# A two-layer trunk kernel: gate rows and routing weight products behind the first expert, first splits between the sort's copies, silu for the expert values

## The reference, cut to what matters

```python
sh1, sc1, g1, sh2, sc2, g2 = modulation(cond, w_mod, b_mod)    # six rows of D per layer and token kind
h2 = rmsnorm(x, norm2_g) * (1 + sc2) + sh2
pg = softmax(h2 @ w_rg + b_rg); pg_top, g_idx = top_k(pg, 1)   # one of 4 groups
le = (h2 @ w_re + b_re).reshape(-1, 4, 4)                       # 4 experts a group
pe_top, e_idx = top_k(softmax(le[group]), 2)                    # 2 experts of the group
combine[t, e] = pe_top / sum(pe_top) * pg_top
hid = silu(h2 @ w_eg[e]) * (h2 @ w_eu[e])                       # for every e of 16, width 256
x = x + g2 * sum_e (hid * combine[:, e]) @ w_ed[e]
```

## Time and profile before

| | |
|---|---|
| median of 3 runs | 2925.8 us (2925.13 to 2928.38) |
| profiled execution | 2934.5 us, span of the trace 2932.6 us |
| PE busy | 2620.1 us (89%) |
| PE weight loads | 1946.5 us (66%) |
| DVE busy | 1571.4 us (54%) |
| ACT busy | 1275.3 us (43%) |
| POOL busy | 38.7 us (1%) |
| read from HBM | 683.6 MB, mean 235 GB/s over the span |
| mean granted clock of PE | 0.936 |

### The profile page before, as it was taken

One profiled execution on the slowest core, in us unless ns is written; L12 is line 12 of the kernel. 1 busy time (PEld: TensorE's weight loads), 2 busy tenths in 40 slices (PEclk: granted clock), 3 DMA queues, 4 the chain that ended last, 5 costly groups with the idle time before them and its releaser, 6 DMA issues. The chain is left out here.

```text
span 2932.6 us, 33895 instructions
## 1 busy us (share of the span) xinstructions
PE 2620.1 (89%) x12386; PEld 1946.5 (66%) x12387; DVE 1571.4 (54%) x2039; ACT 1275.3 (43%) x1720; POOL 38.7 (1%) x68
## 2 busy tenths in 40 slices
PE   6799778999999899888988987789999989798897
PEld 1488434888887475666766873468888868476675
DVE  0444323455454343688885443245454555378887
ACT  0244233434443232666764433334344433267675
POOL 0000000000000002000000000000000000200000
PEclk7799988999999898999988999899999999799998
DMA  9654886555555658678774559755555535368875
GB/s 392 250 194 165 335 322 270 186 189 185 185 190 188 270 203 315 230 290 313 291 273 149 195 211 359 295 227 185 191 185 177 199 110 194 132 231 310 310 295 219
DMA packets 115640, 690.00 MB, mean 235 GB/s; under 512 B 24748, under 2 KB 30668, under 8 KB 32944
## 3 DMA queue, kind: packets, MB, share of 16 engines
q1 hardware_dynamic: 115504, 688.08, 63.2%
HBM read 683.58 MB, written 4.46 MB: 235 GB/s over the span
## 5 line engine op out<-in xcount | busy, mean ns | idle before, releaser
L880 DVE TENSOR_TENSOR low_w<-raw_w,high_w 128x1024 fp32r<-128x1024 f32 (+1 forms) x912 | 1080.2, 1213 | 723.4 <-ACT high_w L554 718.3
L554 ACT ACTIVATE high_w<-raw_w 128x1024 fp32r<-128x1024 f32 (+1 forms) x912 | 938.9, 1051 | 734.6 <-PE bank L1421 669.0
L1419 PE MATMUL bank<-high_w,in_high 128*128 128x512 f32 (+1 forms) x1856 | 724.2, 390 | 20.4 <-DVE low_w L880 20.4
L1420 PE MATMUL bank<-low_w,in_high 128*128 128x512 f32 (+1 forms) x1856 | 720.3, 388 | 0.0
L1421 PE MATMUL bank<-high_w,in_low 128*128 128x512 f32 (+1 forms) x1856 | 720.2, 388 | 0.0
L1419 PEld LDWEIGHTS bank<-high_w,in_high 128*128 128x128 f32 x1856 | 351.7, 189 | 103.7 <-issue 33.8
L1421 PEld LDWEIGHTS bank<-high_w,in_low 128*128 128x128 f32 x1856 | 351.1, 189 | 70.9
L1420 PEld LDWEIGHTS bank<-low_w,in_high 128*128 128x128 f32 x1856 | 351.5, 189 | 69.9
L1439 PE MATMUL bank<-mod_w,cond 128*32 128x512 f32 x1536 | 241.9, 727 | 88.4 <-DMA mod_w<-in_w_mod 81.2
L1768 PE MATMUL bank<-high_w,win_high 128*128 128x512 f32 x512 | 212.0, 414 | 52.9 <-DVE low_w L880 50.2
L1769 PE MATMUL bank<-low_w,win_high 128*128 128x512 f32 x512 | 202.3, 395 | 0.0
(11 more groups left out here) (217 smaller groups left out, 2095.1 us busy)
## 6 DMA issues: line engine op xcount, KB each, us to landing
mod_w<-in_w_mod SPq DMA_DIRECT2D x192, 1024.0 KB, 7.9
raw_w<-in_w_gate SPq DMA_DIRECT2D x128, 1024.0 KB, 4.8
raw_w<-in_w_exp_gate_up SPq DMA_DIRECT2D x128, 1024.0 KB, 4.9
raw_w<-in_w_in SPq DMA_DIRECT2D x64, 1024.0 KB, 4.8
raw_w<-in_w_exp_down SPq DMA_DIRECT2D x64, 1024.0 KB, 5.3
raw_w<-in_w_branch SPq DMA_DIRECT2D x32, 1024.0 KB, 4.8
raw_w<-in_w_out SPq DMA_DIRECT2D x32, 1024.0 KB, 4.8
raw_w<-in_w_in_rest SPq DMA_DIRECT2D x8, 512.0 KB, 3.7
```

The source lines that it names most:

```text
L554: act.activation(high_w[:, part, ks, 0:width], raw_w[:, slot, ks, 0:width], ACT.Copy).then_inc(high_ready, 1)
L880: dve.tensor_tensor(low_w[:, part, ks, 0:width], raw_w[:, slot, ks, 0:width], high_w[:, part, ks, 0:width].bitcast(F32), ALU.subtract).the ...
L1419: pe.matmul(out, highs[:, kk, t, :], high_w[:, part, k, 0:width], start=start, stop=False)
L1420: pe.matmul(out, highs[:, kk, t, :], low_w[:, part, k, 0:width], start=False, stop=False)
```

## The change

- The gate rows leave the routing stage. PE makes one row (`row_step`, a product into `mod_bank`) after the second and after the fourth expert of each group, ACT copies it (`row_copy`) at the end of its iteration for that expert, behind `hid_copy`. POOL waits for the router's products (`routed`) instead of the norm's first part; `diag` and `ones` lie elsewhere.
- The 16 mod units that stood beside gate rows and sort in layer 0 now stand beside `turn_back` (stage "turn back"), four ahead of its third step and two behind each following one, all ahead of the sort.
- The products of the routing weights and the transposes for `unsort` go to `sort_outputs`, behind the first expert's products; their copies are `comb_copy` (DVE, in expert 1 behind the splits of unit 1) and `unsort_copies` (ACT, in expert 1 behind the splits of unit 2). The second transposes go to `mod_bank`.
- In sort steps 3 to 6 ACT and DVE split one half each of the first expert's units 0 and 1 (`split_early`), behind their work on the step. ACT writes `win_high` ahead of `by_slot` and DVE waits for both.
- ACT takes silu instead of sigmoid of the gate values (`gate_values`); DVE multiplies up value, `comb` and that in one pass, and both drains in `hidden` go. `comb_copy` has a drain of its own.
- ACT's second exp of the router stands ahead of all remaining `copy_back`.

The diff, cut to its core:

```diff
-                      "expert rows": [(l + 1, FIRST - 4, FIRST - 2)], "sort": [(l + 1, FIRST - 2, FIRST)]}
+                      "turn back": [(l + 1, FIRST - 4, FIRST)]}
...
+    EARLY = range(3, 3 + SPLIT_SLOTS * HALVES)
...
-        diag = place("diag", [P, 2, COLS], at=region + 8192)
+        diag = place("diag", [P, 2, COLS], at=full_at)
...
+            def split_early(half):
+                if half == 0:
+                    act.wait_ge(raw_in[at.parity("unit", RAW_SLOTS)], at.done(f"in{at.parity('unit', RAW_SLOTS)}") * 16 + 16)
+                slot, part, u = at.parity("unit", RAW_SLOTS), at.parity("unit", SPLIT_SLOTS), at.done("unit")
+                act.wait_ge(unit_used, (u - SPLIT_SLOTS) * HALVES + half + 1)
+                ks = slice(half * HALF, (half + 1) * HALF)
+                act.activation(high_w[:, part, ks, :], raw_w[:, slot, ks, :], ACT.Copy).then_inc(high_ready, 1)
+                if half == HALVES - 1:
+                    at.next("unit")
+                    at.next(f"in{slot}")
...
-                for i in range(2, 4):
-                    copy_back(i)
                 act.wait_ge(route_top, 2 * l + 2)
                 act.activation(route[:, :, 43:44], route[:, :, 43:44], ACT.Exp).then_inc(route_exp, 1)
-                for i in range(4, 2 * KB):
+                for i in range(2, 2 * KB):
                     copy_back(i)
-                gate_rows()
+                mods_done.units += UPC * len(mod_stage(l, "norm") + mod_stage(l, "turn back"))
                 for q in range(NK // 2):
                     act.wait_ge(sort_summed, NK // 2 * l + q + 1)
                     src = banks[2 + q % 2][:, :].rearrange("p (k n) -> p k n", k=2)
-                    act.activation(by_slot[:, 2 * q:2 * q + 2, :], src, ACT.Copy)
                     act.activation(win_high[:, 2 * q:2 * q + 2, :], src[:, :, 0:P], ACT.Copy).then_inc(slots_high, 1)
-                act.wait_ge(unsort_turned, l + 1)
-                for h in range(2):
-                    act.activation(unsort[:, 2 * h:2 * h + 2, :, :].rearrange("p g t n -> p (g t n)"), turn_banks[h][:, :], ACT.Copy).then_inc(unsort_ready, 1)
-                act.activation(unsort_rest[:, :, :].rearrange("p t n -> p (t n)"), banks[4][:, 2 * P:(2 + TILES) * P], ACT.Copy).then_inc(unsort_ready, 1)
-                mods_done.units += UPC * len(mod_stage(l, "norm") + mod_stage(l, "expert rows") + mod_stage(l, "sort"))
-                mods_done()
+                    act.activation(by_slot[:, 2 * q:2 * q + 2, :], src, ACT.Copy).then_inc(slots_kept, 1)
+                    if q == EARLY[0]:
+                        mods_done()
+                    if q in EARLY:
+                        split_early((q - EARLY[0]) % HALVES)
+                def unsort_copies():
+                    act.wait_ge(unsort_turned, l + 1)
+                    for h in range(2):
+                        act.activation(unsort[:, 2 * h:2 * h + 2, :, :].rearrange("p g t n -> p (g t n)"), turn_banks[h][:, :], ACT.Copy).then_inc(unsort_ready, 1)
+                    act.activation(unsort_rest[:, :, :].rearrange("p t n -> p (t n)"), mod_bank[:, 0:TILES * P], ACT.Copy).then_inc(unsort_ready, 1)
+                def row_copy(i):
+                    act.wait_ge(row_summed, at.next("row") + 1)
+                    act.activation(gate_row[:, :, :].rearrange("p t n -> p (t n)")[:, bass.ds(i * COLS, COLS)], mod_bank[:, :], ACT.Copy).then_inc(row_ready, 1)
+                def gate_values(pair, after):
+                    act.wait_ge(unit_used, (at.done("unit") - after) * HALVES)
+                    need(act, chunk_read, at.done("chunk") - 1)
+                    for t in range(TILES):
+                        done = act.activation(sig[:, t, 0:DE], banks[2 * pair + t][:, 0:DE], ACT.Silu)
+                    done.then_inc(gate_ready, 1)
...
+                            if at.first and h == 1 and j == 2:
+                                unsort_copies()
                             if j == 1 and later:
-                                sigmoids((l * LAYER_CHUNKS + LAYER_CHUNKS - DOWN + h + 1) % 2, 2, gate_ready, DE)
+                                gate_values((l * LAYER_CHUNKS + LAYER_CHUNKS - DOWN + h + 1) % 2, 2)
                         hid_copy.bank = (h + 1) % 2
                         if later:
                             hid_copy(g * PER + (h - 1))
                         else:
                             at.next("hid")
+                        if h % 2:
+                            row_copy(g * 2 + h // 2)
...
-                    dve.wait_ge(slots_high, NK // 2 * l + q + 1)
+                    dve.wait_ge(slots_kept, NK // 2 * l + q + 1)
                     src = banks[2 + q % 2][:, :].rearrange("p (k n) -> p k n", k=2)[:, :, 0:P]
                     dve.tensor_tensor(win_low[:, 2 * q:2 * q + 2, :], src, win_high[:, 2 * q:2 * q + 2, :].bitcast(F32), ALU.subtract).then_inc(slots_low, 1)
-                    mod_step(len(mod_stage(l, "sort")) * UPC // (NK // 2))
-                dve.wait_ge(comb_sorted, l + 1)
-                dve.tensor_copy(comb[:, :, :].rearrange("p t e -> p (t e)"), banks[4][:, 0:TILES * NE]).then_inc(comb_taken, 1)
-                mod_step(0)
+                    if q in EARLY:
+                        split_early((q - EARLY[0]) % HALVES)
+                def comb_copy():
+                    dve.wait_ge(comb_sorted, l + 1)
+                    dve.tensor_copy(comb[:, :, :].rearrange("p t e -> p (t e)"), banks[4][:, 0:TILES * NE])
+                    dve.drain()
                 def hidden(pair, e):
                     n = at.next("hidden")
-                    dve.drain()
                     dve.wait_ge(gate_ready, n + 1)
                     need(dve, hid_turned, n)
                     for t in range(TILES):
-                        dve.scalar_tensor_tensor(prod[:, t, 0:DE], banks[2 * pair + t][:, DE:2 * DE], comb[:, t, bass.ds(e, 1)],
-                                                 sig[:, t, 0:DE], ALU.mult, ALU.mult)
-                    dve.drain()
-                    for t in range(TILES):
-                        done = dve.tensor_tensor(prod[:, t, DE:2 * DE], banks[2 * pair + t][:, 0:DE], prod[:, t, 0:DE], ALU.mult)
+                        done = dve.scalar_tensor_tensor(prod[:, t, DE:2 * DE], banks[2 * pair + t][:, DE:2 * DE], comb[:, t, bass.ds(e, 1)],
+                                                        sig[:, t, 0:DE], ALU.mult, ALU.mult)
...
+                mods = len(mod_stage(l, "turn back")) * UPC // (2 * KB)
+                mod_step(mods)
+                mod_step(mods)
                 for i in range(2, 2 * KB):
                     turn_back(i)
-                gate_rows(len(mod_stage(l, "expert rows")) * UPC // (2 * KB), diag, gate_diag_ready)
+                    mod_step(mods)
+                mod_step(0)
...
-                    mod_step(len(mod_stage(l, "sort")) * UPC // (NK // 2))
-                mod_step(0)
-                pe.wait_ge(comb_ready, l + 1)
-                pe.wait_ge(windows_ready, l + 1)
-                for g in range(GROUP_N):
-                    for t in range(TILES):
-                        pe.matmul(banks[4][:, g * PER:(g + 1) * PER], sort_windows[:, t, g, :], comb[:, t, g * PER:(g + 1) * PER], start=t == 0, stop=t == 1)
-                for t in range(TILES):
-                    done = pe.matmul(banks[4][:, NE:2 * NE], sort[:, t, P:2 * P], comb[:, t, :], start=t == 0, stop=t == 1)
-                done.then_inc(comb_sorted, 1)
-                pe.wait_ge(row_ready, at.done("row"))
-                for g in range(GROUP_N):
-                    for t in range(TILES):
-                        turn(turn_banks[g // 2], (g % 2 * TILES + t) * P, sort_windows[:, t, g, :])
-                pe.wait_ge(comb_taken, l + 1)
-                for t in range(TILES):
-                    done = turn(banks[4], 2 * P + t * P, sort[:, t, P:2 * P])
-                done.then_inc(unsort_turned, 1)
                 counts = [pe.value_load(spans[0:1, 1, g * PER:g * PER + 1], min_val=0, max_val=2 * P) for g in range(GROUP_N)]
                 pe.wait_ge(slots_low, NK // 2 * (l + 1))
-                pe.wait_ge(unsort_ready, 3 * (l + 1))
+                def sort_outputs():
+                    pe.wait_ge(comb_ready, l + 1)
+                    pe.wait_ge(windows_ready, l + 1)
+                    for g in range(GROUP_N):
+                        for t in range(TILES):
+                            pe.matmul(banks[4][:, g * PER:(g + 1) * PER], sort_windows[:, t, g, :], comb[:, t, g * PER:(g + 1) * PER], start=t == 0, stop=t == 1)
+                    for t in range(TILES):
+                        done = pe.matmul(banks[4][:, NE:2 * NE], sort[:, t, P:2 * P], comb[:, t, :], start=t == 0, stop=t == 1)
+                    done.then_inc(comb_sorted, 1)
+                    for g in range(GROUP_N):
+                        for t in range(TILES):
```

(15 more changed lines are left out.)

42 lines of the change are left out of this document (32 added, 10 removed).

## The result

The changed kernel takes 2938.3 us (2936.16 to 2948.86), 1.0044 of the kernel before [1.003, 1.0058]: slower by 0.44%, on a chip on which the kernel before took 2927.09 us. By the same ratio that is 2938.7 us beside the 2925.8 of before; forecast were 2928.0, in a range of 2910 to 2948, with no change that can be measured as the likeliest. The time lies in the range, but above the 2931.7 from which the prediction calls the kernel slower, which it had given 34%.

What follows compares the result with a forecast made beforehand. Bounds: the routing stage, where TensorE waits, and the expert loop, with TensorE busy 88% and VectorE 86 to 87%. Terms: +30.8 - 22.9 - 7.9 = 0.0, plus 2 for small waits: 2925.8 + 2 = 2928 us, range 2910 to 2948.

Steps and rivals of the forecast that it cites:

- Silu: Expert loop: one pass without drains cuts an expert from 13.05 to 11.99 us, 16.5 us a layer won, 33 in all.
- The far end of 1 us an expert: ScalarE in the expert loop: extra table loads if silu shares no table with the copies; priced at 0, few chances in 100.
- Gate rows in the loop: Expert loop: ScalarE's row copy holds back the next expert's splits, 3.5 us a row, 26 us a layer lost, 52 in all.
- Clock: TensorE after 2.9 us idle at rows: 1.4 us a fall, two or three falls, 2.5 us a layer lost.
- slow clock: Rival, expert loop: nearly every row followed by the half clock, 16 x 1.4 = 22 us instead of 5, 2945 us; 20%.
- `sort_outputs` in the loop: First expert: routing weight products moved into TensorE's stream in the loop cost 3.4 us a layer.
- The 4.6 that the seam gave: Layer 1, between sort and first expert product: first two units split earlier, TensorE needs about 1 us, 4.6 us won.
- Routing of layer 1: Sort starts 18.7 us earlier without gate rows, 4.6 won after it, up to 0.4 lost: 22.9 us won.
- Routing of layer 0: 16 mod units consumed ahead of the sort at 422 GB/s: first expert product 7.9 us earlier, bounds 1 to 9.
- Sum: Both expert stages +30.8, layer 1 routing -22.9, layer 0 routing -7.9: 0.0 us, before 2 us for small waits.
- port: Rival: GpSimd's `diag` work blocks VectorE's splits through a shared SBUF port, 2932 to 2940 us, 2935; 13%.

Runs made afterwards that it cites:

- experiment 1: Kernel before the change with only silu and one VectorE pass without drains in `hidden`: 2897.67 us, 0.9865 of the kernel before.
- experiment 3: Changed kernel with the gate row product moved ahead of the last unit of the expert, ScalarE's copy left in place: 2887.28 us, 0.9839 of the kernel before.
- experiment 4: Changed kernel with two further TensorE products, results unused, behind each gate row product: 2928.17 us, 0.9977 of the kernel before.
- experiment 5: Changed kernel with only ScalarE's row copy put off to behind the next expert's gate values: 2872.47 us, 0.9796 of the kernel before.
- experiments 8 to 10: Experiment 3 without early splits: 2891.76 us; experiment 5 with `sort_outputs` and its copies ahead of the loop: 2881.20 us; experiment 5 with both: 2890.39 us.
- experiment 6: Experiment 3 with a row product of 4 columns instead of 512, so gate rows are wrong: 2879.21 us, 0.982 of the kernel before.
- experiment 7: Experiment 3 with GpSimd writing each diagonal twice: 2892.78 us, 0.987 of the kernel before.
- experiment 2: Changed kernel with sigmoid, both VectorE passes and both drains back: 2971.44 us, 1.0112 of the kernel before.

## Why the prediction came out as it did

*Silu*: right by itself. Forecast intervals of 11.99 us and 16.5 us a layer; 11.9 and 16.4 to 17.6 in experiment 1. The far end of 1 us an expert, for a table that changes, didn't come: one table load a layer stands at the line of silu in after (columns: busy us, mean ns):

```profile
L824 ACT ACT_TABLE_LOAD x2 | 2.6, 1283 | 0.0
```

*Gate rows in the loop*: mechanism and bare size right, shown by experiments 3, 4 and 5. 3.5 us a row was forecast from the chain product, copy, split, `low_w`; 3.6 was measured in experiment 4. The places are those that were named: ScalarE at `row_copy`, VectorE at the next half, TensorE at `low_w`. Its idle behind a row without pieces was forecast as 2.9 us and is 3.0; it is 4.04 in the rows shown above, where the next expert begins with a window piece on both other engines, a case that the working had left aside:

```profile
2726.00 1.02 PE L1782 MATMUL bank<-diag,ones 128*128 128x512 f32 x2
2730.01 0.50 PE L1826 MATMUL bank<-high_w,win_high 128*128 128x512 f32 x1 [2.99 <-DVE low_w L915]
```

*Clock*: the step that failed. It said "1.4 us a fall, two or three falls, 2.5 us a layer". In the trace of after 13 of the 14 row intervals hold a stretch at the half clock, and eight of these stretches are twice as long as the one in the earlier trace rows, like this one in layer 0:

```profile
1278.00:1284.80 6.80, 6.17 (x15) 4.83 (x16) 5.99 (x7) 4.41 (x7) 2.09 (x1) 0.50 0.55 201
```

A plain row interval lies above its 15.5 us by 1.4 to 1.6 us with a short one and by 2.8 to 2.9 with a long one; one with pieces lies above the 17.8 of experiment 4 by 0.4 to 0.6 and by 1.4 to 1.5. By the stages, against experiment 4, that is 12.5 and 9.0 us a layer. Two errors: the count was drawn from one fall and one that didn't come, and the price from that one fall, as if the next had to be as short. The rival "slow clock", at 20%, had the mechanism and by luck the total (16 x 1.4 = 22, measured 21.5): fewer falls inside the loops, some longer, some nearly hidden. The time lies between its 2945 and the forecast, as the first expert gave something back (below).
The Trainium skill ("TensorE: Matmul & The Clock Gate", section "HAM oscillation — how this bites in real kernels") says that a loop whose TensorE waits some 3 to 5 us at each tile pays for the fall anew at each tile, not once. This case's loops agree (13 of 14, after 3.0 to 4.2 us); read beside the earlier trace rows it would have been reason to give that rival more than 20%.

*`sort_outputs` in the loop*: 3.4 us a layer were counted, and in the trace of after it is 3.2 (2591.34 to 2594.54). The 4.6 that the seam gave were put down to both moves together; by experiments 8 to 10 the early splits have nearly all of it, and `sort_outputs` 1 us at most.

*Routing of layer 1*: 22.9 forecast, 22.5 measured.

*Routing of layer 0*: 7.9 forecast, 2.5 measured, inside its bounds of 1 to 9. The rate of the transfers was well chosen (413 GB/s from 1135 to 1165). But the sort began at 1170.38 instead of 1168.5: the last unit's product started only at 1166.82, and its copy and turns took 3.6 us more, in part at a low clock. The sort's own first steps ran at it too (16.95 us against 14.37 in layer 1), and the first expert product came 2.6 us behind the sort.

*Sum*: by stages the forecast was 0.0 and the traces give 15.8 us. 5.4 come from layer 0's routing, 0.4 from layer 1's, 5.7 and 4.3 from the loops. There the clock took 21.5 us, and 1.4 of them the one fall of the earlier trace rows had taken in before too: 15.1 more than the 5 that were counted. The first expert gave some back: from its first product to the first `hid_low` it is 23.8 us in after and 22.5 in experiment 1, 1.3 us a layer where 3.4 were counted. The products of `sort_outputs` did cost their 3.2; but in experiment 1, as in before, TensorE starts the first expert at the half clock (4.0 us of it, 2.0 lost) and in after it doesn't. The prediction did not have that, and in experiments 3, 5 and 6 it does start so in four of six places: that after is spared it is luck. The larger misses apart from this one all made the kernel slower, and that the time still lies between 2910 and 2948 is owed to the breadth of the range more than to the sum. The 2 us for "port" and small waits were not needed in the loop (experiment 7).

## What to carry to other kernels

Before you move work into a loop that has slack on every engine, look at what each in-order queue holds behind the new wait: eight copies of 0.5 us cost this loop 3.6 us each, because the next expert's splits stood behind them, and 0.4 us each once they stood behind something that is late anyway. When a move makes TensorE idle for some us, price the clock at every such place and for more than one length of the fall, not by the one fall that a trace happened to show. The gain was there from the start: with that one ScalarE instruction half an expert later, the same change takes 2872.47 us, 0.9796 of the kernel before.

## What the runs showed of the hardware

- TensorE's clock, 1.2 instead of 2.4 GHz after idle times of 3.0 and 4.0 us at a row, cost up to 2.9 us a place, twice what one fall in before had cost. How often the clock fell at or behind an idle time of TensorE: 12 of 12 times at 3.8 to 4.2 us and 14 of 16 times at 3.0 us (rows of after and experiment 2), 4 of 14 times at 2.6 to 2.7 us (first expert products of after and experiments 2 to 7), once in 6 at 2.1 to 2.5 us and never in 8 at 1.3 us (rows of experiment 4, where two more products stand ahead of the idle). Experiment 4, with the same waits but two more products in each, ran at 1.00 and 0.99: useless products made the kernel 0.7% quicker.
- GpSimd beside VectorE: 0.60 us alone, 0.87 as a mean in the loop of layer 1 in experiment 3, 1.55 in experiment 5, 1.73 for the second writing in experiment 7, with VectorE's splits at 1.222 us in experiment 3 and 1.226 in the other two. The Trainium skill ("SBUF — State Buffer", "SBUF: two separate sides") has the engine that comes second wait for the whole instruction of the other. The split reads two operands from SBUF, the case that the rule names, and twice as much GpSimd work doesn't lengthen it: here GpSimd gave way and the splits did not, and the measurement decides.
